# Order of the turns inside a group of weight chunks, and another table of modulation sums, in a two-block transformer kernel

## The chip, the cores and the metric

The kernel runs on one core of one Trainium2 chip. The metric is device time in microseconds (us) of one execution. Five engines work side by side: PE (TensorE, matrix multiplication), DVE (VectorE), ACT (ScalarE), POOL (GpSimd) and SP (SyncE, which here only issues the loads of weights). They share data through on-chip buffers and wait for each other on semaphores. Each engine executes its own instructions strictly in the order in which they are written, so an instruction that waits holds up everything behind it.

## The reference

Two transformer blocks on 256 tokens of width 2048, in float32. The first:

```
mod = silu(c) @ w_ada + b_ada                     # 2048 x 12288: six vectors: shifts, scales, gates
h = modulate(rms_norm(x), sh_a, sc_a)             # the same for the 256 context tokens
qa, kva, kr, cb, cc, ch = split(h @ w_in)
att = attention(8 heads, keys of x and of the context)      # softmax, q and k through low-rank products
conv = cb * dwconv3(cc * ch)                      # depthwise over three neighbouring tokens
x = x + gt_a * (rms_norm(concat(att, conv)) @ w_out)
hf = modulate(rms_norm(x), sh_f, sc_f)
u = dwconv3(hf @ w_up); a, g = split(u)
x = x + gt_f * ((a * silu(g)) @ w_down)
```

The second block has two other attentions of 8 heads each, a gated merge and a squared-ReLU MLP of width 8192. The time is that of streaming some 550 MB of weights through PE.

## The kernel before

**Weights in chunks.** SP loads a weight as chunks of 512 KB (2 tiles of 128 rows, 512 columns each) into the ring `raw` of 8 slots. A matrix product in float32 accuracy is made of three products of reduced precision: ACT rounds a chunk into `whi` (`split`, L613), DVE computes `wlo = raw - whi` (`split`, L1093), and PE multiplies `whi` by the rounded activations, `whi` by their rest, and `wlo` by the rounded ones (`block`, L1869 to L1871). `whi` and `wlo` have rings of 4 slots (`NSPLIT`), so ACT can be at most four chunks ahead of PE. A chunk is 24 matmuls of 256 columns.

**Groups.** A product of 512 output columns is a group of 8 chunks (some have 6 or 4). While PE multiplies group k, ACT and DVE already split group k+1. Both walk it in a function `ahead(group, between, later, sums, side, third)` of their own. Its loop over the chunks n puts other work of these engines ahead of a chunk's split:

- `between`, at n = 4: the output of group k is taken out of PE's accumulator (the line that copies or scales `half`), with what follows directly.
- `later`, at n = 6: the rest of its treatment, such as `gated` (SiLU gate and product into `hid`) in the first block's FFN.
- `side[n]`: one step of work that runs in the background. `att1` is a step of the first attention: on DVE the maximum over a head's scores (L1457) and sometimes a `mix` (L1462), on ACT the squares of an older head's output (L828), a copy (L833), the exponential (L837), and the scaled copy of an older head's output (L843).
- `sums`: after the split of chunk n, `sum_chunks` takes so many chunks of `w_ada` and adds them, scaled by silu(c), to `acc` (DVE L1120 or L1122 for one half and L1125 for the other). Eight of them make 512 modulation values. PE then reduces `acc` over the partitions (`mod`, L1840) and DVE's `mod` adds them to `mod_f`.

The attention is a round trip: PE computes a head's scores into one bank (L2122, L2123), DVE takes the maximum (L1457), ACT the exponential into `tmp` (L837), and only then may PE compute the next scores. The root that scales a head (POOL L575 to L583) starts from L828's sum and ends at ACT's L843. PE does these steps between two products' chunks.

**Stages.** To about 140 us `w_ada`'s first third and the norm, from 140 to 555 us the projections, convolution and first attention, to 601 us the rest of `w_out` and the FFN's norm (`ffn_norm` on DVE, in the group that carries UP_SUMS[0]), to 975 us the 16 products with `w_up` that stand in straight code, then loops: the other `w_up` products and `w_down`. The second block starts at about 1380 us. The remaining two thirds of `w_ada`'s chunks are summed in the stages between; 32 of them in the `w_up` stage, by the table `UP_SUMS` (one tuple for each product, one number for each chunk n). `UP_MODS` says after which products' gates DVE adds the four finished sums. The same tables set the order in which SP loads, since `raw` is one ring for all.

Of the kernel before, what the change touches and what calls it, by code (L numbers as in the profile page):

```python
# [16 lines left out]
GC = KT // KC  # L17
# [151 lines left out]
FIRST_TILES = (8, 9, 10, 11, 0, 1, 2, 3, 12, 13, 14, 15)  # L169
LAST_TILES = (4, 5, 6, 7)  # L170
WIDE_SUMS = (2, 1, 1, 2, 1, 1)
LIGHT, HEAVY, NONE = (0, 0, 1, 1, 0, 0, 1, 1), (0, 0, 0, 1, 0, 0, 0, 0), (0,) * GC
UP_SUMS = [NONE] + [LIGHT, HEAVY] * 6 + [(0, 0, 1, 1, 0, 0, 0, 0)] + [NONE] * 2
UP_MODS = (8, 16, 20, 28)
FILLS = [("x", tb, q) for tb in range(2) for q in range(4)] + ["roots"] + \
    [("ctx", tb, q) for tb in range(2) for q in range(4)] + ["vec a", "vec b"]
FILL_AT = list(range(10, 18)) + [33] + list(range(38, 46)) + [46, 47]
# [10 lines left out]
def program(nc, ins, consts, out, known, traced):  # L188
    with ExitStack() as ctx:
# [216 lines left out]
        def _(sp):  # L406
# [71 lines left out]
            def up_group(c0, sums):  # L478

                for c, count in enumerate(sums):  # L480
                    load(W["w_up"], KC * c, KC, c0, GW)
                    load_mod(count)

            for t in range(0, 2 * HT, 4):
                up_group(t * P, UP_SUMS[t // 2])
                up_group(FFN + t * P, UP_SUMS[t // 2 + 1])

# [115 lines left out]
        def _(act):  # L603
# [3 lines left out]
            def split(elems):  # L607

                act.wait_ge(raw_in[L.raw_slot()], L.loads())
                if L.n.get("hi_ready", 0) >= NSPLIT:  # L610
                    act.wait_ge(s_chunk_used, L.at("hi_ready", 1 - NSPLIT))
                s, c = L.split_slot(), L.raw_slot()
                A(whi[:, s, 0:elems], raw[:, c, 0:elems], ACT.Copy).then_inc(s_hi_ready, 1)  # L613
                L.mark("hi_ready")
                L.add("drained")
# [13 lines left out]
            def per(sums, n):  # L629
                return sums if isinstance(sums, int) else sums[n]  # L630

            def ahead(group, between=None, later=None, sums=0, side=None, third=None, split=split):


                L.end = L.n.get("hi_ready", 0)
                chunks = group
                for n, elems in enumerate(chunks):
                    if third and n == third[0]:
                        third[1]()
                    if side and n in side:  # L640
                        next(side[n], None)
                    if n == 4 and between:
                        between()
                    if n == 6 and later:
                        later()
                    split(elems)
                    L.add("drained", per(sums, n))
                if len(chunks) <= 4 and between:
                    between()
                if len(chunks) <= 4 and side and 4 in side:  # L650
                    next(side[4], None)
                if len(chunks) <= 6 and later:
                    later()
# [38 lines left out]
            def norm(name, src, dst, shift=None, known=False, after=None):  # L692
                if not known:
                    squares(flat(src), after=after)
                    root(T, rstd[:, 0:T], D)
                round_tiles(name, KT, lambda k: dst[:, k, 0:T], shift)


            for name in ("c", "c_ctx", "b_ada"):
                g, r, n = VEC_AT[name]  # L700
# [192 lines left out]
            def into_ffn(g):  # L893
                turn()
                act.wait_ge(s_half_read, L.at("half_read"))
                square_x(g)

            def ffn_root():
                root_of(rstd[:, 0:T], sum_bank[:, 0:T], D, ("sq", L.n["squared_x"] - 1), "ffn")

            ahead(LAST, turn)
            for g in range(3):
                ahead(LAST, lambda: into_ffn(g))
            ahead(STD, lambda: (into_ffn(3), ffn_root(), norm("hf", xt, hf, lambda k: mod_f[:, 16 + k:17 + k], True)), None, UP_SUMS[0])

# [6 lines left out]
            def up(side, tile, nb=4):  # L912

                turn()
                act.wait_ge(s_half_read, L.at("half_read"))
                for b in range(nb):
                    taps(("ffn_conv_w1", "ffn_conv_b"), tile + (FT * side + b), b, conv_y[side][:, b, :], side)
# [14 lines left out]
            for t in range(0, 2 * HT, 4):  # L932
                ahead(STD, lambda: up(0, t), None, UP_SUMS[t // 2 + 1])
                ahead(STD, lambda: up(1, t), lambda: gated(t // HT, t % HT), UP_SUMS[t // 2 + 2] if t < 2 * HT - 4 else 0)
            with L.loop(2):
# [67 lines left out]
            for s in range(4):  # L1003
                before = att[s - 1] if s > 0 else None
                side = [{} if before is None else d for d in ({6: before}, {1: before, 4: before, 6: before}, {1: before, 4: before})]
# [78 lines left out]
        def _(dve):  # L1084
# [44 lines left out]
            def per(sums, n):  # L1129
                return sums if isinstance(sums, int) else sums[n]  # L1130

            def ahead(group, between=None, later=None, sums=0, side=None, third=None, split=split):


                L.end = L.n.get("hi_ready", 0)
                chunks = group
                for n, elems in enumerate(chunks):
                    if third and n == third[0]:
                        third[1]()
                    if side and n in side:  # L1140
                        next(side[n], None)
                    if n == 4 and between:
                        between()
                    if n == 6 and later:
                        later()
                    split(elems)
                    sum_chunks(per(sums, n))
                if len(chunks) <= 4 and between:
                    between()
                if len(chunks) <= 4 and side and 4 in side:  # L1150
                    next(side[4], None)
                if len(chunks) <= 6 and later:
                    later()
# [102 lines left out]
            for g in range(8):  # L1256
                ahead(STD, mod_rows if g > 0 else None, (lambda: mod_cols(4 * g - 4)) if g > 0 else None,
                      side={c: replies[GC * g + c] for c in range(GC) if GC * g + c in replies})
# [254 lines left out]
            def both(*parts):  # L1513
                for part in parts:
# [8 lines left out]
                  side={1: att1, 3: rotate(3), 4: conv_normed(1, 0), 5: both(conv_normed(1, 1))}, third=(1, lambda: keys(3)))  # L1523
# [8 lines left out]
            def into_ffn(g):  # L1532
                onto_x(4 * g, mix_gate)
                L.add("squared_x")
# [13 lines left out]
            for g in range(1, 3):  # L1548
                ahead(LAST, lambda: into_ffn(g))
            ahead(STD, ffn_norm, None, UP_SUMS[0])  # L1550

# [23 lines left out]
            for t in range(0, 2 * HT, 4):  # L1575
# [3 lines left out]
                ahead(STD, lambda: up(1, t),  # L1579
                      lambda: (gated(t // HT, t % HT, 4, key), mod() if t + 4 in UP_MODS else None), 0 if last else UP_SUMS[t // 2 + 2])  # L1580
            with L.loop(2) as i:
# [123 lines left out]
            for s in range(4):  # L1705
# [3 lines left out]
                      side={2: roots()} if s == 0 else {1: before, 4: before, 6: before})  # L1709
                ahead(STD, lambda: (times(k2[:, s % 2, :, :], rr, ("k", s)), token_roots() if s == 0 else None),  # L1710
                      (lambda: norm_x(0 if s == 0 else 3)) if s < 2 else None,
                      side={} if s == 0 else {1: before, 4: before})
# [103 lines left out]
        def _(pe):  # L1816
# [399 lines left out]
            for t in range(0, 2 * HT, 4):  # L2216
                product(of(hf), ready=(lambda n: ("hf", n)) if t == 0 else None, with_mod=t in UP_MODS, sums=UP_SUMS[t // 2])
                product(of(hf), sums=UP_SUMS[t // 2 + 1])
# [167 lines left out]
```

## Time and profile before

| | before |
|---|---|
| runs | 2724.72, 2726.81 and 2737.24 us, median 2726.81 |
| execution that was profiled | 2737.24 us, its span 2735.5 us |
| PE busy | 2643.3 us, 97% of the span |
| DVE busy | 1737.7 us, 64% |
| ACT busy | 1224.1 us, 45% |
| POOL busy | 110.0 us, 4% |
| chain that ended last | PE 87%, DVE 7%, ACT 2%, POOL 1% |

The profiled execution is the slowest of the three, 10.4 us above the median. Busy time is a sum over stages with different limits, and PE counts as busy at half clock as well. The chain that ended last is followed back from the last instruction: at each step to what released it.

### The profile page before, as it was taken

How to read it: one execution, taken by the hardware profiler on the slowest of the kernel's cores; microseconds unless marked ns; L12 is line 12 of the kernel's file. 1: busy time of each engine (PE TensorE's matmuls, PEld its weight loads, DVE VectorE, ACT ScalarE, POOL GpSimd, SP SyncE). 2: the span in 40 equal slices, each digit the busy share in tenths (PEclk: the TensorE clock that was granted, in tenths of full speed). 3: DMA queues.
4: the chain of work that ended last, by engine and by line, in shares of the span. 5: the costliest groups of instructions: out<-in, count | busy, mean ns of one | idle time of the engine just before them, and what ended most of it. 6: DMA issues, size and time to landing. Idle time of an engine off the chain costs nothing.

```text
span 2735.5 us, 51222 instructions
## 1 busy us (share of the span) xinstructions
PE 2643.3 (97%) x21440; PEld 2560.4 (94%) x21440; DVE 1737.7 (64%) x2020; ACT 1224.1 (45%) x1487; POOL 110.0 (4%) x196
## 2 busy tenths in 40 slices
PE   6899988989999999999999999999999999999998
PEld 4699877889999999999999999999999999999997
DVE  5988676777888755665564555555555555555554
ACT  6743333345454544444543444444444444434433
POOL 0000323300000000000000010000000000000000
PEclk9999999999999999999998999999999999999999
DMA  9877766747777655465564555666556656666662
GB/s 355 276 233 263 244 207 206 244 165 239 250 237 251 212 190 185 155 222 180 172 193 132 163 161 162 193 188 198 184 178 194 194 193 195 194 193 190 196 208 100
DMA packets 289064, 553.56 MB, mean 202 GB/s; under 512 B 19386, under 2 KB 28712, under 8 KB 288232
## 3 DMA queue, kind: packets, MB, share of 16 engines
q1 hardware_dynamic: 288328, 548.53, 61.9%
q8 instruction: 142, 2.33, 0.3%
q10 hardware_dynamic: 544, 2.29, 0.2%
q14 instruction: 50, 0.41, 0.0%
HBM read 548.53 MB, written 2.10 MB: 201 GB/s over the span
## 4 chain that ended last, share of the span: by engine, by line
PE 87%; DVE 7%; ACT 2%; issue 2%; POOL 1%; DMA 1%; SPq 0%; ACTq 0%; DVEq 0%; POOLq 0%
PE half L1869 26%; PE half L1870 26%; PE half L1871 26%; DVE wlo L1093 3%; PE half L1903 1%; PE half L1905 1%; PE half L1904 1%; PE half L2162 1%; ACT whi L613 1%; DVE acc L1122 1%; DMA raw<-in_w_ada 1%; DVE acc L1125 1%; PE half L2123 0%; PE half L2150 0%; PE half L2122 0%
## 5 line engine op out<-in xcount | busy, mean ns | idle before, releaser
L1093 DVE TENSOR_TENSOR wlo<-raw,whi 128x1024 fp32r<-128x1024 f32 (+1 forms) x909 | 1090.9, 1211 | 829.8 <-ACT whi L613 827.3
L613 ACT ACTIVATE whi<-raw 128x1024 fp32r<-128x1024 f32 (+1 forms) x909 | 942.2, 1049 | 1077.6 <-PE half L1871 946.7
L1869 PE MATMUL half<-hf,whi 128*128 128x256 f32 x2400 | 670.3, 279 | 6.2 <-DVE hf L1185 5.1
L1870 PE MATMUL half<-hf,whi 128*128 128x256 f32 x2400 | 668.8, 279 | 0.0
L1871 PE MATMUL half<-hf,wlo 128*128 128x256 f32 x2400 | 668.8, 279 | 0.0
L1869 PE MATMUL half<-hid,whi 128*128 128x256 f32 x1712 | 475.6, 278 | 0.0
L1871 PE MATMUL half<-hid,wlo 128*128 128x256 f32 x1712 | 475.0, 277 | 0.0
L1870 PE MATMUL half<-hid,whi 128*128 128x256 f32 x1712 | 474.9, 277 | 0.0
L1869 PEld LDWEIGHTS half<-hf,whi 128*128 128x128 f32 x2400 | 452.5, 189 | 7.7 <-issue 5.8
L1870 PEld LDWEIGHTS half<-hf,whi 128*128 128x128 f32 x2400 | 453.2, 189 | 0.0
L1871 PEld LDWEIGHTS half<-hf,wlo 128*128 128x128 f32 x2400 | 453.1, 189 | 0.0
L1869 PE MATMUL half<-h,whi 128*128 128x256 f32 x1520 | 431.7, 284 | 5.1 <-issue 3.8
L1870 PE MATMUL half<-h,whi 128*128 128x256 f32 x1520 | 425.8, 280 | 0.0
L1871 PE MATMUL half<-h,wlo 128*128 128x256 f32 x1520 | 425.4, 280 | 0.0
L1871 PEld LDWEIGHTS half<-hid,wlo 128*128 128x128 f32 x1712 | 322.8, 189 | 0.0
L1869 PEld LDWEIGHTS half<-hid,whi 128*128 128x128 f32 x1712 | 321.7, 188 | 0.1
L1870 PEld LDWEIGHTS half<-hid,whi 128*128 128x128 f32 x1712 | 321.6, 188 | 0.1
L1869 PEld LDWEIGHTS half<-h,whi 128*128 128x128 f32 x1520 | 289.5, 190 | 7.1 <-issue 4.6
L1870 PEld LDWEIGHTS half<-h,whi 128*128 128x128 f32 x1520 | 290.0, 191 | 0.6 <-issue 0.2
L1871 PEld LDWEIGHTS half<-h,wlo 128*128 128x128 f32 x1520 | 289.6, 190 | 0.0
L1125 DVE SCALAR_TENSOR_TENSOR acc<-raw,silu_sb,acc 128x512 f32<-128x512 f32 x128 | 96.2, 752 | 4.5
L1122 DVE SCALAR_TENSOR_TENSOR acc<-raw,silu_sb,acc 128x512 f32<-128x512 f32 x112 | 84.3, 753 | 12.0 <-DVE wlo L1093 0.5
(284 smaller groups left out, 3064.7 us busy)
## 6 DMA issues: line engine op xcount, KB each, us to landing
raw<-in_w_up SPq DMA_DIRECT2D x288, 512.0 KB, 4.4
raw<-in_w_in SPq DMA_DIRECT2D x216, 512.0 KB, 4.0
raw<-in_w_down SPq DMA_DIRECT2D x212, 512.0 KB, 4.7
raw<-in_w_ada SPq DMA_DIRECT2D x192, 512.0 KB, 5.3
raw<-in_w_out SPq DMA_DIRECT2D x64, 512.0 KB, 5.0
raw<-in_w_proj_a SPq DMA_DIRECT2D x16, 512.0 KB, 4.3
raw<-in_w_proj_b SPq DMA_DIRECT2D x16, 512.0 KB, 4.1
raw<-in_w_up SPq DMA_DIRECT2D x16, 384.0 KB, 3.4
```

The costliest lines, as they stand in the source:

```text
L613: A(whi[:, s, 0:elems], raw[:, c, 0:elems], ACT.Copy).then_inc(s_hi_ready, 1)
L1093: V.tensor_tensor(wlo[:, s, 0:elems], raw[:, c, 0:elems], whi[:, s, 0:elems].bitcast(F32), ALU.subtract).then_inc(s_drained, 1)
L1122: V.scalar_tensor_tensor(a, w[:, 0, :], s[:, 0:1], a, ALU.mult, ALU.add).then_inc(s_dve_step, 1)
L1125: V.scalar_tensor_tensor(a, w[:, 1, :], s[:, 1:2], a, ALU.mult, ALU.add).then_inc(s_drained, 1)
L1869: mm(o, hi, x[:, 0:T], start=(k == 0 and b % 2 == 0), stop=False, skip_group_check=True)
L1870: mm(o, hi, x[:, T:2 * T], start=False, stop=False, skip_group_check=True)
L1871: return mm(o, lo, x[:, 0:T], start=False, stop=(k == nk - 1), skip_group_check=True)
L1903: mm(o, xh, hi, start=(k == 0), stop=False)
L1904: mm(o, xh, lo, start=False, stop=False)
L1905: ins_ = mm(o, xl, hi, start=False, stop=(k == nk - 1))
L2162: ins_ = mm(sum_bank[:, i * T:(i + 1) * T], ones[:], sq[:, n % 2, b * T:(b + 1) * T], start=(first and i + b == 0), stop=(last and b == 3) ...
```

## The change

Three edits. In the tables, the 32 `w_ada` chunks of the `w_up` stage are spread otherwise: before, products in pairs had four chunks (at n = 2, 3, 6, 7) and one (at n = 3), from the second group on; after, each of the first ten groups has three (at n = 1, 3, 5), the eleventh two, and the last five none. The group of `ffn_norm` is the first of them and had none before. `UP_MODS` follows. In ACT's `ahead`, the background step `side[n]` stands behind `between` and `later` where it stood ahead of both. In DVE's, it stands behind `between`, still ahead of `later`. PE's and POOL's functions are as they were.

```diff
-LIGHT, HEAVY, NONE = (0, 0, 1, 1, 0, 0, 1, 1), (0, 0, 0, 1, 0, 0, 0, 0), (0,) * GC
-UP_SUMS = [NONE] + [LIGHT, HEAVY] * 6 + [(0, 0, 1, 1, 0, 0, 0, 0)] + [NONE] * 2
-UP_MODS = (8, 16, 20, 28)
+UP_SUMS = [(0, 1, 0, 1, 0, 1, 0, 0)] * 10 + [(0, 1, 0, 0, 0, 1, 0, 0)] + [(0,) * GC] * 5
+UP_MODS = (8, 12, 16, 24)
 # ACT, ahead():
                     if third and n == third[0]:
                         third[1]()
-                    if side and n in side:
-                        next(side[n], None)
                     if n == 4 and between:
                         between()
                     if n == 6 and later:
                         later()
+                    if side and n in side:
+                        next(side[n], None)
                     split(elems)
 # DVE, ahead():
                     if third and n == third[0]:
                         third[1]()
+                    if n == 4 and between:
+                        between()
                     if side and n in side:
                         next(side[n], None)
-                    if n == 4 and between:
-                        between()
                     if n == 6 and later:
                         later()
```

The changed file is one line shorter above all functions, so its line numbers are those of before less one. The edits to `ahead` take effect where a group has both a turn at n = 4 and `side[4]`.

DVE, in the group whose turn is `conv_in(4)` (about 397 us; `convt` and `zpad` are the convolution's buffers), before:

```order
L1125 SCALAR_TENSOR_TENSOR acc<-raw,silu_sb,acc 128x512
L1457 TENSOR_REDUCE stat<-half 128x1
L1462 SCALAR_TENSOR_TENSOR mix<-half,vec,mix 128x256
L1159 TENSOR_TENSOR zpad<-half,sq 128x4x256
L1380 MEMSET stat 128x1
L1385 SCALAR_TENSOR_TENSOR convt<-zpad,vec,convt 128x256 x4
L1390 SCALAR_TENSOR_TENSOR convt<-zpad,vec,convt 128x256 x4
L1093 TENSOR_TENSOR wlo<-raw,whi 128x1024
```

The same place after:

```order
L1124 SCALAR_TENSOR_TENSOR acc<-raw,silu_sb,acc 128x512
L1158 TENSOR_TENSOR zpad<-half,sq 128x4x256
L1379 MEMSET stat 128x1
L1384 SCALAR_TENSOR_TENSOR convt<-zpad,vec,convt 128x256 x4
L1389 SCALAR_TENSOR_TENSOR convt<-zpad,vec,convt 128x256 x4
L1456 TENSOR_REDUCE stat<-half 128x1
L1461 SCALAR_TENSOR_TENSOR mix<-half,vec,mix 128x256
L1092 TENSOR_TENSOR wlo<-raw,whi 128x1024
```

The maximum over the scores, and with it the round trip to PE, moved behind ten convolution instructions. On ACT the four taps of the convolution moved ahead of the attention's step in the same place. In the group that starts at about 300 us (turn `conv_in(2)`), ACT has before:

```order
L828 ACTIVATE r,stat<-half 128x128
L833 ACTIVATE sq<-half 128x512
L837 ACTIVATE tmp,stat<-half,stat 128x512
L843 ACTIVATE r<-half,stat 128x128
L794 ACTIVATE zpad<-convt 128x4x256
```

and after:

```order
L793 ACTIVATE zpad<-convt 128x4x256
L827 ACTIVATE r,stat<-half 128x128
L832 ACTIVATE sq<-half 128x512
L836 ACTIVATE tmp,stat<-half,stat 128x512
L842 ACTIVATE r<-half,stat 128x128
```

The copy into `zpad` moved ahead of the whole attention step; on DVE the `convt` product moved ahead of the maximum there. In three other places such turns change places: one copy of a `row` at about 87 us, the values `vt` at about 456 us, and in the second block q, k, v and the gate's sigmoid against steps of its attentions.

DVE at the end of `ffn_norm`'s group and in the first group with a gate (`hid`), in the `w_up` stage, has after the change:

```order
L1092 TENSOR_TENSOR wlo<-raw,whi 128x1024 x2
L1121 SCALAR_TENSOR_TENSOR acc<-raw,silu_sb,acc 128x512
L1124 SCALAR_TENSOR_TENSOR acc<-raw,silu_sb,acc 128x512
L1553 COPY zpad<-half 128x4x256
L1357 SCALAR_TENSOR_TENSOR sq<-zpad,vec,sq 128x256 x4
L1362 SCALAR_TENSOR_TENSOR sq<-zpad,vec,sq 128x256 x4
L1092 TENSOR_TENSOR wlo<-raw,whi 128x1024 x2
L1119 TENSOR_SCALAR acc<-raw,silu_sb 128x512
L1124 SCALAR_TENSOR_TENSOR acc<-raw,silu_sb,acc 128x512
L1158 TENSOR_TENSOR sq<-sq 128x1024
L1158 TENSOR_TENSOR hid<-sq,hid 128x4x256
```

where before the two `wlo` were followed directly by the gate:

```order
L1554 COPY zpad<-half 128x4x256
L1358 SCALAR_TENSOR_TENSOR sq<-zpad,vec,sq 128x256 x4
L1363 SCALAR_TENSOR_TENSOR sq<-zpad,vec,sq 128x256 x4
L1093 TENSOR_TENSOR wlo<-raw,whi 128x1024 x2
L1159 TENSOR_TENSOR sq<-sq 128x1024
L1159 TENSOR_TENSOR hid<-sq,hid 128x4x256
```

A summed chunk (n = 5) now stands between the turn and the gate, in five of the eight groups that have a gate.

## Rows read from the trace of the kernel before

**Rows 1.** The page: busy time of PE, and the chain by engine.

```profile
PE 2643.3 (97%) x21440; PEld 2560.4 (94%) x21440; DVE 1737.7 (64%) x2020; ACT 1224.1 (45%) x1487; POOL 110.0 (4%) x196
PE 87%; DVE 7%; ACT 2%; issue 2%; POOL 1%; DMA 1%; SPq 0%; ACTq 0%; DVEq 0%; POOLq 0%
```

**Rows 2.** Timeline of DVE from 392 us: start, duration, instruction [idle before].

```profile
397.17 0.68 DVE L1457 TENSOR_REDUCE stat<-half 128x1 f32<-128x512 f32 x1
400.66 1.22 DVE L1159 TENSOR_TENSOR zpad<-half,sq 128x1024 f32<-128x1024 f32 x1
...
406.25 1.22 DVE L1093 TENSOR_TENSOR wlo<-raw,whi 128x1024 fp32r<-128x1024 f32 x1
```

**Rows 3.** Timeline of ACT from 392 us.

```profile
394.26 0.25 ACT L828 ACTIVATE r<-half 128x128 f32<-128x128 f32 x1
...
397.89 0.69 ACT L837 ACTIVATE tmp<-half,stat 128x512 f32<-128x512 f32 x1 [2.80 <-DVE stat L1457]
...
399.49 0.37 ACT L843 ACTIVATE r<-half,stat 128x128 f32<-128x128 f32 x1 [0.82 <-POOL stat L583]
...
402.03 2.08 ACT L789 ACTIVATE convt<-zpad,vec 128x256 f32<-128x256 f32 x4 [1.81 <-DVE stat L1380]
```

**Rows 4.** Timeline of PE from 398 us.

```profile
398.73 2.08 PE L2122 MATMUL half<-ktt,qall 128*128 128x512 f32 x2 [4.87 <-ACT tmp L837]
```

**Rows 5.** A window by engine: length, busy (instructions), granted clock, DMA share, GB/s.

```profile
397.00:407.20 10.20, 8.47 (x25) 5.47 (x26) 7.00 (x14) 6.21 (x13) 2.99 (x8) 0.50 0.32 99
```

**Rows 6.** Timeline of DVE from 300 us.

```profile
303.67 0.68 DVE L1457 TENSOR_REDUCE stat<-half 128x1 f32<-128x512 f32 x1
304.27 1.21 DVE L1159 TENSOR_TENSOR convt<-half,convt 128x1024 f32<-128x1024 f32 x1
```

**Rows 7.** Timeline of ACT from 300 us.

```profile
301.11 0.28 ACT L828 ACTIVATE r<-half 128x128 f32<-128x128 f32 x1 [3.92 <-PE half L2150]
...
304.39 0.69 ACT L837 ACTIVATE tmp<-half,stat 128x512 f32<-128x512 f32 x1 [2.42 <-DVE stat L1457]
...
305.99 0.37 ACT L843 ACTIVATE r<-half,stat 128x128 f32<-128x128 f32 x1 [0.82 <-POOL stat L583]
306.25 1.05 ACT L794 ACTIVATE zpad<-convt 128x1024 f32<-128x1024 f32 x1
```

**Rows 8.** Timeline of PE from 306 us.

```profile
306.79 1.02 PE L2122 MATMUL half<-ktt,qall 128*128 128x512 f32 x2
```

**Rows 9.** Timeline of DVE from 585 us, in the norm's group.

```profile
588.35 1.22 DVE L1093 TENSOR_TENSOR wlo<-raw,whi 128x1024 fp32r<-128x1024 f32 x1 [2.03 <-ACT whi L613]
589.50 0.15 DVE L1159 TENSOR_TENSOR mod_f<-half,vec 128x4 f32<-128x4 f32 x1
...
596.90 1.75 DVE L1543 RECIPROCAL rstd<-rstd 128x256 f32<-128x256 f32 x1 [5.47 <-ACT rstd L799]
```

**Rows 10.** Timeline of DVE from 646 us, in the first group with a gate.

```profile
649.78 1.23 DVE L1093 TENSOR_TENSOR wlo<-raw,whi 128x1024 fp32r<-128x1024 f32 x1 [1.60 <-ACT whi L613]
651.11 0.75 DVE L1122 SCALAR_TENSOR_TENSOR acc<-raw,silu_sb,acc 128x512 f32<-128x512 f32 x1
...
652.57 1.22 DVE L1554 COPY zpad<-half 128x1024 f32<-128x1024 f32 x1
...
663.88 4.63 DVE L1093 TENSOR_TENSOR wlo<-raw,whi 128x1024 fp32r<-128x1024 f32 x4
```

**Rows 11.** Timeline of ACT from 646 us.

```profile
648.69 1.06 ACT L613 ACTIVATE whi<-raw 128x1024 fp32r<-128x1024 f32 x1 [1.77 <-PE half L1871]
```

**Rows 12.** Windows, L1869 alone: length, PE busy (matmuls), PEld busy, clock, DMA.

```profile
844.00:891.00 47.00, 38.12 (x138) 25.82 (x138) 1.00 0.73 244
931.00:1154.00 223.00, 177.20 (x630) 118.29 (x630) 1.00 0.56 181
1160.00:1297.00 137.00, 111.20 (x403) 75.62 (x403) 1.00 0.58 197
```

**Rows 13.** The window at half clock, columns as in rows 5.

```profile
1485.90:1503.00 17.10, 17.10 (x81) 17.10 (x82) 2.94 (x6) 2.05 (x4) 0.00 (x0) 0.50 0.30 95
```

## The prediction

> **What bounds the kernel now.** I read the page first. PE is busy for 2643.3 us, 97% of the span, and the chain that ended last lies on PE for 87%, on DVE for 7% [rows 1]. So DVE's and ACT's orders cost nothing as long as PE finds its next chunk ready, and the change can act in three ways only: where PE runs dry while it waits for DVE or ACT, where the rounds of the attention make it wait, and by the pace of its own matmuls. I then went to each place where the order of the two engines differs, and read DVE, ACT and PE there side by side.
>
> The worst is at 397 us. The chain there is DVE's maximum at 397.17, ACT's exponential at 397.89, PE's scores at 398.73, and PE had idled 4.87 us for it [rows 2 to 4]. The reader is to see that a single short instruction, well placed, ends a stall of PE, and that `conv_in(4)` stood behind it, from 400.66 on, where nobody waited for it.
>
> **The place at 397 us.** `conv_in(4)` now goes first. On DVE it takes from 400.66 to 406.25, 5.6 us, taps of ACT included [rows 2]; its input is there, since PE had ended the product before it turned idle (398.73 - 4.87 = 393.9) [rows 4]. The maximum moves from 397.17 to about 402.8, the exponential to 403.5, the scores to 404.3: PE's stall grows from 4.9 to 10.5 us. On ACT the taps come before the attention's step, and the square sum L828 can't start before they end: 397.17 + (402.03 - 400.66) + 2.08 = 400.6 instead of 394.26. From L828 to the scaled copy L843 it was 5.2 us [rows 3], so L843 comes at 405.8, 1.5 us behind the scores where before it was 0.8 behind: some 0.5 us more may show. I take **+5.6**. Bounds: 0 if the product in front were later than I think and PE had no turn there, 7 if L843 is late as well. The split behind it comes at 407 instead of 406.3, and it is for a chunk that PE reaches some chunks later. The half clock after the stall was 10.2 us [rows 5]: granted 0.50, that is 1.2 GHz, behind an idle stretch of 4.9 us. A longer idle stretch before it need not lengthen what follows the restart; I add **0.5**, between 0 and 4.
>
> **The place at 304 us.** PE took up the scores at 306.79 without a wait [rows 8]. DVE's `convt` (1.21 us) now precedes the maximum, 303.67 becomes 304.9, and ACT's `zpad` copy, which needs `convt`, holds L828 to L843 back until 305.9 [rows 6, 7]. The exponential starts at about 306.85 and lasts 0.69, scores at 307.7: +0.9. Worse, L828 moves from 301.11 to 305.9, L843 was 4.9 behind it, so it comes at 310.8 where it was 305.99, and PE's turn for that head follows the scores by 3 us. PE waits there 1.4 us more. **+2.3**, bounds 0 and 5.
>
> **Other exchanges.** At 456 us `vt` (1.2 us) goes ahead of work behind which DVE idled long for PE; at 87 us a row copy exchanges with a product of equal rank; in the second block the steps of the attention are turned against 1.2 us copies where I found no wait of PE at all. **0** for all, bounds -1 and +2; the cover is the four split chunks that PE has in hand.
>
> **The norm's group.** The group of `ffn_norm` had no sums, and has two before the turn. DVE idled 2.03 us before the split at 588.35, which hides the first. The second falls between that split and `mod_f` at 589.50, and from there everything is serial: squares, root on ACT, reciprocal at 596.90, `hf`, PE [rows 9]. A summed chunk costs DVE 652.57 - 651.0 = 1.6 us with its issue [rows 10]. **+1.6**, bounds 0 (if the sum fell into the wait as the first does) and 3.
>
> **The gated groups.** In the first group with a gate, ACT's split of chunk 3 starts at 648.69, released by PE's end of the group before [rows 11]. So PE needs chunk 6 six chunks later. A chunk is 24 matmuls of 223 / 1890 = 0.118 us, 2.83 us [rows 12], which gives 665.7. DVE starts that split (the first of the four at 663.88) and ends it at 665.1 [rows 10]: between them stand the turn, two splits, the gate. With the semaphores the margin is some 0.3 us. The change puts one more sum between, 1.6 (1.4 where it is the first of eight). Followed in the same way, the five gated groups that get it have margins of 0.3, 0.9, 0.3, 1.1 and 1.4. Stalls: 1.1 + 0.7 + 1.3 + 0.5 + 0.2 = 3.8, and what the pairs before had too much in the ungated groups gives 0.3 back, while a stall in one group moves the ring for the next; I take **+4**, bounds 0 and 8. It is no matter of loads: eleven chunks of 0.52 MB in 22.6 us are 255 GB/s, and where 244 GB/s were moved the share of the DMA engines was 0.73 [rows 12], so it becomes 0.76.
>
> **PE's pace.** At full clock PE has two paces. From 931 to 1154 us there are 630 matmuls of one line out of three in 223 us, 0.1180 us each; from 844 to 891 us 138 in 47 us, 0.1135; and from 1160 to 1297 us 403 in 137 us, 0.1133 [rows 12]. The granted clock is 1.00 in all three. The pace changes only where the stream is interrupted: by the sums' matmuls (L1840) at four places in the `w_up` stage, or by a stall. Four such places gave fast, slow, fast, slow, and the last one holds for 223 us. Of the 553 us from 601 to 1154, 111 were fast (89 about the stretch of the row, and 22 from 705 on, found in the same way). The change moves these places to products 4, 6, 8 and 12 and adds stalls, so the draw is made anew. All slow costs 111 x (0.118 / 0.1133 - 1) = +4.6; all fast gains 442 x 0.04 = -17. The largest stake is the stretch behind the last place, some 260 us or 10 us. I take half of it: **-5**.
>
> By the Trainium skill (TensorE: Matmul & The Clock Gate, Back-to-back issue gap) isolated back-to-back matmuls are N / 2.4 + 2.5 ns apart at the full clock, one value for 256 columns, 109 ns. The rows have 113 and 118 at the same granted clock, so the page doesn't give the second pace; were one rate all there is, this term would be 0 and the time 2741.
>
> **Sum.** 5.6 + 0.5 + 2.3 + 0 + 1.6 + 4 - 5 = +9.0. The profiled execution took 2737.24 us, but 17.1 us of it ran at half clock with PE busy all through and no stall before [rows 13], 8.5 us lost. Without it: 2728.7, 1.9 above the median of 2726.8; I set the sum against the median: **2736 us**.
>
> **Rivals.** (a) *The pace falls to slow and stays.* Place: behind the last sums, product 12, at about 895 us. If the stream restarts slow there and in the earlier pieces, the term is +4.6 instead of -5 and the time 2726.8 + 14.0 + 4.6 = 2745, slower. It decides as soon as less than about 130 us of the 553 run fast. For it: 442 of 553 us were slow. Against: 630 us further on are fast for long after interruptions of the same kind.
> (b) *The round trips are absorbed.* PE has work between its attention steps, and a stall of one round shortens the next: L843 or the next wait comes with its own slack. Then 304 and 397 us cost 2 together, the gates 1, the norm 0: 2726.8 + 3 - 3 = 2727. For it: after the place at 397 there are further waits that another engine sets. Against: those are set by PE's own progress and move along.
> (c) *The pace is fast from the norm on.* -17 instead of -5, 2724; with (b) besides, 2712.
> (d) *The stalls cost more than their length.* Each of the gated stalls resets the pace or takes the clock to 0.50 for as long as at 397 us, 4 us a time at one or two places, and L843's lateness is carried: 2750.
>
> **How the numbers follow.** Forecast 0.43; (a) 0.24; (b) 0.14; (c) 0.11, a third of it below 2713; (d) 0.08. About 0.5%, 13.6 us, is what a measurement of this kernel can tell from no change: faster means under 2713.2, slower over 2740.4. Slower: (a) and (d) wholly or nearly, 0.30. Faster: the third of (c) and a little of (b), 0.06. The rest, 0.64, is the same. Range: 2721 to 2749, which leaves about 0.08 on each side; the forecast's own is 2730 to 2741.
>
> **What would show it.** PE's wait for the exponential at about 404 us should be 10 to 11 us, DVE's maximum there behind the convolution. At about 311 us PE should wait for L842. DVE's `mod_f` in the norm should stand 1.6 us later after the split than now. The gated groups should show gaps of 0.2 to 1.3 us before PE's chunk 6. The interval of PE's matmuls behind 895 us tells the pace. I am wrong if the wait at 404 us is still 5 us, if the time until 601 us is not 9 to 10 us longer, or if between 601 and 1160 us the difference is outside -13 to +9.

## The result, and the profile after

| | before | after |
|---|---|---|
| median | 2729.4 us (4 runs, 2724.7 to 2737.2) | 2751.2 us (4 runs, 2749.6 to 2753.3) |
| profiled execution, span | 2737.2, 2735.5 us | 2751.8, 2749.9 us |

The fourth run of before, 2732.0 us, was not known when the forecast was made. The ratio is 1.0078, with a 95% interval of 1.0051 to 1.0104. The forecast was 2736 us in a range of 2721 to 2749: the time lies 2 us above the range. The page of the changed kernel has PE at nearly the busy time of before and a larger part of the chain on DVE, 9% against 7 [rows 1]:

```profile
PE 2646.2 (96%) x21440; PEld 2561.8 (93%) x21440; DVE 1738.6 (63%) x2020; ACT 1224.0 (45%) x1487; POOL 102.9 (4%) x196
PE 84%; DVE 9%; ACT 2%; issue 2%; DMA 1%; POOL 1%; SPq 0%; ACTq 0%; DVEq 0%; POOLq 0%
```

**At 397 us** DVE's timeline shows the convolution ahead of the maximum, which answers to [rows 2]:

```profile
398.34 1.22 DVE L1158 TENSOR_TENSOR zpad<-half,sq 128x1024 f32<-128x1024 f32 x1
...
403.93 0.68 DVE L1456 TENSOR_REDUCE stat<-half 128x1 f32<-128x512 f32 x1
```

ACT's timeline has the exponential right behind it, and the scaled copy L842 1.4 us behind the exponential [rows 3]; PE's timeline has the wait, 8.7 us where it was 4.9 [rows 4]:

```profile
404.65 0.69 ACT L836 ACTIVATE tmp<-half,stat 128x512 f32<-128x512 f32 x1 [2.13 <-DVE stat L1456]
...
406.10 0.37 ACT L842 ACTIVATE r<-half,stat 128x128 f32<-128x128 f32 x1 [0.67 <-POOL stat L582]
```

```profile
405.48 1.22 PE L2121 MATMUL half<-ktt,qall 128*128 128x512 f32 x1 [8.68 <-ACT tmp L836]
```

From the start of `zpad` to that of the maximum it is 5.6 us, the term of the sum to the tenth.

**At 304 us** PE waits for the scores, which it did not before [rows 8]:

```profile
304.48 0.70 PE L2121 MATMUL half<-ktt,qall 128*128 128x512 f32 x1 [3.73 <-ACT tmp L836]
```

For the scaled copy L842, for which the forecast had a second wait there, PE did not wait: ACT's row is the first of these, PE's the second.

```profile
306.50 0.37 ACT L842 ACTIVATE r<-half,stat 128x128 f32<-128x128 f32 x1 [2.07 <-POOL stat L582]
308.45 0.42 PE L2139 MATMUL half<-ident_sb,r 128*128 128x128 f32 x1
```

**In the norm's group** a summed chunk stands between the split and `mod_f`, and DVE's idle time before the split went from 2.03 to 0.94 us [rows 9]:

```profile
596.06 1.23 DVE L1092 TENSOR_TENSOR wlo<-raw,whi 128x1024 fp32r<-128x1024 f32 x1 [0.94 <-ACT whi L612]
597.39 0.75 DVE L1121 SCALAR_TENSOR_TENSOR acc<-raw,silu_sb,acc 128x512 f32<-128x512 f32 x1
...
598.85 0.15 DVE L1158 TENSOR_TENSOR mod_f<-half,vec 128x4 f32<-128x4 f32 x1
```

From the split to `mod_f` it is 2.8 us, where it was 1.15. PE's wait for ACT's squares in the norm grew by the same 1.6 us, here before and then after:

```profile
PE half L2162 <- ACT sq L885: 3.6, 1, 3.6
PE half L2161 <- ACT sq L884: 5.2, 1, 5.2
```

**In the gated groups** PE waits for `wlo` five times from 603 to 900 us, where before had no such wait at all. PE's waits there:

```profile
PE half L1868 <- DVE wlo L1092: 3.1, 5, 0.9
```

So a stall of PE stands at each of the four places that the prediction named. At 304 us the second wait that it had there is missing. To see what the places cost in all I cut both traces at the same matmul of PE; each trace has 21,440 of them, in the same order but for those of L1840. Since PE has two paces, I also price every fast matmul as a slow one: I add 0.0045 us for each that runs at 0.1133 us. I call this the priced time. Two priced times of the same stretch differ by waits and half clock only. Later executions of the same two kernels are in the table as well (labels are those of the experiments below); the columns are the stretches by before's clock.

```
               127-   284-   388-   456-   584-   602-    fast matmuls  profiled
               284    388    456    584    602    1160    in all        execution, us
before         159.0  105.6   68.3  129.9   17.7  562.7   12368         2737.2
e1, same       157.4  105.5   68.3  129.5   17.7  563.0   11864         2737.0
e16, same      159.0  105.8   64.5  129.5   17.1  562.7   11704         2735.4
after          157.8  111.0   72.4  130.0   19.3  567.5   12094         2751.8
e5, same       157.4  107.7   71.5  127.9   19.3  565.9   11873         2746.8
e13, same      157.1  107.9   72.8  130.0   19.3  568.0   13481         2743.5
e14, same      156.8  107.9   71.5  128.9   19.2  567.3   12998         2744.6
e15, same      157.1  104.7   73.1  129.5   19.3  567.7   11842         2746.9
mean after
- mean before   -1.3   +2.2   +5.3   -0.3   +1.8   +4.5
```

Behind 1160 us the priced times are 255.5 and 1053.6 us in all eight for two stretches, and 298.9 to 302.2 for the one between.

### The profile page after: what moved, and what is told of

Its sections match the earlier page's. It is cut to its first block, busy times and chain, and to the rows that moved or that the text cites. A ratio compares the mean times of both kernels' runs of the same rounds, so it can differ in the third digit from the quotient of the medians.

```text
span 2749.9 us, 51222 instructions
## 1 busy us (share of the span) xinstructions
PE 2646.2 (96%) x21440; PEld 2561.8 (93%) x21440; DVE 1738.6 (63%) x2020; ACT 1224.0 (45%) x1487; POOL 102.9 (4%) x196
## 4 chain that ended last, share of the span: by engine, by line
PE 84%; DVE 9%; ACT 2%; issue 2%; DMA 1%; POOL 1%; SPq 0%; ACTq 0%; DVEq 0%; POOLq 0%
PE half L1868 25%; PE half L1869 25%; PE half L1870 25%; DVE wlo L1092 3%; DVE acc L1121 1%; DMA raw<-in_w_ada 1%; ACT whi L612 1%; PE half L1902 1%; PE half L1904 1%; PE half L1903 1%; DVE acc L1124 1%; PE half L2161 1%; PE half L1991 0%; PE half L2122 0%; PE half L2149 0%
## 5 line engine op out<-in xcount | busy, mean ns | idle before, releaser
L1869 PE MATMUL half<-hf,whi 128*128 128x256 f32 x2400 | 667.5, 278 | 0.0
L1869 PE MATMUL half<-hid,whi 128*128 128x256 f32 x1712 | 476.1, 278 | 0.0
L1868 PEld LDWEIGHTS half<-hf,whi 128*128 128x128 f32 x2400 | 452.3, 188 | 11.3 <-issue 5.8
L1869 PEld LDWEIGHTS half<-hf,whi 128*128 128x128 f32 x2400 | 451.8, 188 | 0.0
L1869 PE MATMUL half<-h,whi 128*128 128x256 f32 x1520 | 425.4, 280 | 0.0
L1869 PEld LDWEIGHTS half<-hid,whi 128*128 128x128 f32 x1712 | 321.4, 188 | 0.1
L1869 PEld LDWEIGHTS half<-h,whi 128*128 128x128 f32 x1520 | 289.7, 191 | 0.6 <-issue 0.2
L1121 DVE SCALAR_TENSOR_TENSOR acc<-raw,silu_sb,acc 128x512 f32<-128x512 f32 x112 | 84.3, 753 | 11.7
```

The costliest lines, as they stand in the source:

```text
L1121: V.scalar_tensor_tensor(a, w[:, 0, :], s[:, 0:1], a, ALU.mult, ALU.add).then_inc(s_dve_step, 1)
L1868: mm(o, hi, x[:, 0:T], start=(k == 0 and b % 2 == 0), stop=False, skip_group_check=True)
L1869: mm(o, hi, x[:, T:2 * T], start=False, stop=False, skip_group_check=True)
```

## The experiments

For each, the ratio is to runs of before made in the same session, with its 95% interval. "Priced" stands for the priced time of a stretch of the table. S and P are the two theories of the expectations: the time was lost in stalls (S), or in the pace of PE's matmuls (P).

**e1 and e16: before again.**

> The kernel before once more, for a second profile of it. Theory S (stalls): the change lost about 14 us in stalls of PE, and the two profiles of before and after (2737.2 and 2751.8) differ by just these 14.5 us; a second profile of before then has the same paces of PE in the same stretches (slow from 931 to 1154 us, 0.118 us a matmul, fast from 1160 to 1297, 0.113). Theory P (pace): the paces are drawn anew in each execution, which is why before spans 2724.7 to 2737.2 us; then the second profile has other stretches fast, and its time differs from 2737.2 by 0.0045 us for every matmul of another pace. The half clock of 17 us at about 1486 us, which I took for an accident: S and P alike, it is there again if it belongs to the program (the changed kernel shows 13.7 us of it in the same place), and gone if my prediction was right.

> The kernel before, a third profile: by P1 and P2 alike fast behind the last sum with a chance of 3 in 8.

Medians 2732.6 (12 runs, 2721.7 to 2737.0; ratio 1.0006, 0.9992 to 1.0020) and 2732.1 us (8 runs). The windows of e1 behind the last sum and in the loop after it, L1869 alone:

```profile
926.00:1152.00 226.00, 179.74 (x641) 120.10 (x640) 1.00 0.58 179
1154.00:1296.00 142.00, 113.00 (x402) 75.46 (x402) 1.00 0.59 191
```

The second is 142 / (3 x 402) = 0.1177 us for a matmul, and the same instructions of the same kernel ran at 0.1133 in the first profile [rows 12]. So the pace is drawn anew in each execution; up to 1409 us this one draw makes 5.8 us. Theory P is right in this. And the half clock at 1486 us is there again, PE busy all through it:

```profile
1486.00:1503.00 17.00, 17.00 (x81) 17.00 (x82) 2.52 (x5) 2.61 (x4) 0.00 (x0) 0.50 0.30 97
```

All 18 profiles have it there or a few us beside, 13.7 to 20.5 us long. It is no accident of the one execution [rows 13], and the 8.5 us that the prediction took off for it were wrong.

**e2: the tables alone.**

```diff
-UP_SUMS = [NONE] + [LIGHT, HEAVY] * 6 + [(0, 0, 1, 1, 0, 0, 0, 0)] + [NONE] * 2
-UP_MODS = (8, 16, 20, 28)
+UP_SUMS = [(0, 1, 0, 1, 0, 1, 0, 0)] * 10 + [(0, 1, 0, 0, 0, 1, 0, 0)] + [(0,) * GC] * 5
+UP_MODS = (8, 12, 16, 24)
```

> Only the tables UP_SUMS and UP_MODS are changed, the order inside the groups is that of before. Theory S: the time to the norm is that of before, the norm's group costs 1.7 us (in the two profiles the step from the product before the norm to the one after it grew by that), the gated groups' stalls some 4 us: +6, ratio 1.002. Theory P: in the changed kernel's profile PE ran at the slow pace from the last sum on to 1425 us, and in that of before it was fast from 1160 to 1297 and in one piece behind it; if the place of the last sum does that, this kernel has it too and costs 6 us more, +12, ratio 1.0045.

Ratio 1.0038 (1.0024 to 1.0051), +10.4 us. Priced: 19.3 in the norm's stretch and 567.7 in the next, 1.8 and 4.9 more than before, and 105.6 and 68.3 ahead of them, as before. So the tables own these two terms, and neither of the other two. The loop from 1160 was fast, against P. The time lies 4 us above S's 6, just outside the interval's half width of 3.6, and 1.6 below P's 12; the priced stretches leave no room for more stalls. What is left is the pace of the runs without a profile, which no trace shows; the profiled run itself had more fast matmuls than before's first.

**e3: the order alone, on both engines.**

> Only the order inside the groups is changed (both engines), the tables are those of before. Theory S: all of the 9 us that are lost before 601 us, of which about 4 at the place at 304 us and 4 at the place at 397 us, and nothing behind: +8 to +9, ratio 1.003. Theory P: the same stalls, and on top of them other paces behind; the time is then anywhere from -8 to +5 beside it.

Ratio 1.0043 (1.0028 to 1.0058), +11.7 us. Its edit is the diff of the two `ahead` functions. Priced: 108.0 and 70.1, then 17.7 and 562.5: the loss is ahead of 601 us and nothing behind. PE's wait for the scores at 304 us is 0.7 us here, by its timeline:

```profile
305.17 1.13 PE L2122 MATMUL half<-ktt,qall 128*128 128x512 f32 x2 [0.69 <-ACT tmp L837]
```

That is the 0.9 of the prediction; in the changed kernel's first profile it was 3.7. The windows tell why: here PE was granted 0.53 of its clock ahead of the place,

```profile
292.00:299.00 7.00, 6.87 (x19) 3.89 (x20) 5.67 (x7) 2.91 (x4) 0.00 (x0) 0.53 0.88 293
```

so it reached the scores later and waited less. In the changed kernel's first profile the clock fell behind the longer wait instead:

```profile
305.00:312.00 7.00, 7.00 (x25) 4.96 (x24) 3.91 (x5) 3.12 (x6) 2.28 (x6) 0.54 0.24 73
```

Of the other profiles with the new order there, e6, e8, e11 and e12 also have 111 us for this stretch, e5, e7, e13 and e14 have 107.7 to 107.9 like e3, and e15 has 104.7. The old order has such draws too. In e4 and e9, where no half clock came ahead of the place, PE waited 1.5 us at these scores, and the stretch took about 107 us in e4, 104 in e9 and 108 in e10. So the two ranges overlap, and only their means, some 3 us apart over seven and eleven profiles, tell the order's part. By the wait alone it is 2.2 us without half clock ahead (3.7 against 1.5), and 0.5 to 0.7 with it. The order on one engine alone was not tried: as the program is written, the two would wait for each other for ever. With DVE alone in the new order its maximum stands behind work that needs taps which ACT has behind this maximum's exponential; with ACT alone in it DVE's L1462, ahead of `zpad`, waits for ACT's L848, which stands behind the taps of that `zpad`.

**e4: the place at 397 us alone.** In before, a parameter makes both engines take the new order in the group of `conv_in(4)`.

```diff
-    ahead(STD, lambda: conv_in(4), ..., side={..., 4: att1, 6: att1})
+    ahead(STD, lambda: conv_in(4), ..., side={..., 4: att1, 6: att1}, new=True)
```

> Only the group whose turn is conv_in(4), at 397 us, has the new order on both engines; everything else is before. Theory S, by the prediction: PE's wait for the exponential grows from 4.9 us to 10.5, +5.6. By the changed kernel's profile, where the step over this place grew by 4.0 us: +4. A rival: the time that PE loses here is given back at the next wait, which another engine's chain sets: 0.

Ratio 1.0020 (1.0009 to 1.0031), +5.5 us. Priced, 388 to 456 us took 70.2, against 68.3, 68.3 and 64.5 in before. It costs, so the rival falls; whether 4 or 5.6 the interval can't tell. PE waited 7.4 us at the scores there, 3 less than forecast. Half clock explains the gap: it came at 377.8 us for 6.8 us, so PE reached the scores some 3.4 us later than at full clock (an estimate from these 6.8 us), while the wait ended when DVE's maximum and the exponential were done. Sorted by how long PE was at half clock just ahead of the place (between 377 and 391 us), the waits of all profiles with these two orders are, in us:

| half clock just ahead | old order at 397 us | new order |
|---|---|---|
| none | 4.7 to 4.9 (before, e1, e2) | 10.3 (e15) |
| 3.4 us | 3.1 (e11) | 8.7 to 8.9 (after, e5 to e8, e13, e14) |
| 6.8 us | 1.6, 1.8 (e16, e12) | 7.2, 7.4 (e3, e4) |

In each row the new order has 5.4 to 5.8 us more. PE's line in e15:

```profile
399.39 2.08 PE L2121 MATMUL half<-ktt,qall 128*128 128x512 f32 x2 [10.27 <-ACT tmp L836]
```

**e11 and e12: the place at 304 us alone, and the changed kernel without the one at 397.** The same parameter, in e11 at `conv_in(2)` of before; e12 is the changed kernel with the old order at `conv_in(4)`.

> Only the group whose turn is conv_in(2), at 304 us, has the new order on both engines. Theory S: the stretch 284 to 388 us, 105.6 us at the slow pace in before, becomes 107.9 where PE was at half clock just ahead of the place (as in e3_order and e7_norm_free), and 111 where it was not (as in the changed kernel's profile); at 601 us less of it is left, since DVE, which sets the time of the scores at 397 us, was late by only 1.2: +1 to +3. Rival: it adds fully: +2.3 to +5.4.

> The changed kernel with only the group at 397 us in the order of before. Theory S: the step from 388 to 405 us is 17.7 us again instead of 21.7, and 601 us is reached 4 to 5.6 us earlier; the stretches behind are those of the changed kernel (567.5 us from the norm to the loops, at the slow pace). Rival (the wait is given back later): no difference at 601 us.

e11: ratio 1.0015 (1.0003 to 1.0028), +4.1 us. Priced 111.0 and 65.7: 5.4 more than before in the stretch of the change and less in the next. e12: ratio 1.0050 (1.0037 to 1.0063), 5 runs; 111.0 and 64.9, against 111.0 and 72.4 in the changed kernel. The step from 388 to 405 us is 11.2 us here, as in e16 (11.3), where the two other profiles of before have 17.6. The reader is to see two things. Of the 7 us between e12 and the changed kernel the order at 397 us makes some 5.6, by the table of waits, for e12 had 6.8 us of half clock ahead of the place and the changed kernel's first profile 3.4. And what PE loses ahead of 397 us is in part taken back there, because PE waits for DVE anyway. But e12's median is not below the changed kernel's (ratio 1.0042 in e5): on the whole time this undoing can't be seen.

**e5, e13, e14, e15: the changed kernel again.**

> The changed kernel once more, for a second profile and the spread of its times. Counted by the number of the matmul, and with every fast matmul (0.1133 us) priced as a slow one (0.1178), the changed kernel's profile is 13 to 15 us longer than the two of before: this part I call the stalls. The medians differ by 21.8. Theory P1: the rest of some 7 us is the pace, drawn from the same distribution as before; five runs in 3.7 us were chance, and more runs of the same kernel scatter over some 15 us as those of before do, with a median of about 2745. Theory P2: in the changed kernel the long stretch behind the last sum's matmuls (896 to 1169 us, 2316 matmuls, 10 us between the paces) is slow in all or nearly all executions; then the runs stay between 2746 and 2755 and the second profile is slow there too.

> The changed kernel, a third profile. P2: slow (0.118 us a matmul) all through the stretch behind the last sum. P1: fast with a chance of 3 in 8.

> The changed kernel, a fourth profile: slow behind the last sum by P2, fast with a chance of 3 in 8 by P1.

> The changed kernel, a fifth profile: slow behind the last sum by P2, fast with a chance of 3 in 8 by P1.

Medians 2744.7 (11 runs, 2737.9 to 2748.9), 2746.3 (8), 2744.8 (7) and 2747.2 us (4); ratios 1.0042 (1.0026 to 1.0059), 1.0045 (1.0032 to 1.0058), 1.0037 (1.0018 to 1.0055) and 1.0039 (0.9995 to 1.0083). So over 30 more runs the change costs 10 to 12 us, not 21.8. The first four after lie 4 to 6.5 us above these medians; those of before, 2729.4, are among the medians of their later sessions, 2728.4 to 2734.8. The 11 runs of e5 scatter over 11 us, as P1 has it. The stretch behind the last sum was slow in all five profiles of the changed kernel. Its windows in the first one:

```profile
897.00:1168.00 271.00, 215.56 (x768) 143.94 (x767) 1.00 0.58 181
```

0.1176 us for a matmul. Over all kernels: with the last sum in product 12, slow in 9 of 9 profiles; with it in product 14 fast in 3 of 9 (e3, e4, e10). In e10:

```profile
932.00:1146.00 214.00, 173.68 (x631) 118.19 (x630) 1.00 0.61 187
```

0.1130 us. None of nine would come in 3 cases of 100 if the chance were one in three; but were the chance the same for both kinds, all three fast ones would still fall among the same nine in 10 cases of 100, so P2 may hold and is not shown.

**e6: the third sum behind the gate.**

```diff
-UP_SUMS = [(0, 1, 0, 1, 0, 1, 0, 0)] * 10 + [(0, 1, 0, 0, 0, 1, 0, 0)] + ...
+UP_SUMS = [(0, 1, 0, 1, 0, 0, 0, 1)] * 10 + [(0, 1, 0, 0, 0, 0, 0, 1)] + ...
```

> The changed kernel with each product's third sum moved from n = 5 to n = 7, behind the gate. Theory S: the gated groups' stalls go (the stretch from the norm to the loops, priced at the slow pace, is 567.6 us in both kernels with the new tables and 562.5 to 563.1 in the four of before's tables): 563 here, time 4 to 5 us less than that of the changed kernel. Rival: the stalls come from having three sums in every gated group, not from where they stand: 567.

Priced, 602 to 1160 us took 562.9 instead of 567.5, and PE's waits there shrank from five and 3.1 us to

```profile
PE half L1868 <- DVE wlo L1092: 0.2, 1, 0.2
```

with the same three sums in the same groups. It is the place of the sum between turn and gate, as the prediction had it. In the whole time (ratio 1.0040, 1.0024 to 1.0057) the 4.6 us don't show: the profile had 11296 fast matmuls, 800 fewer than the changed kernel's first, which is 3.6 us.

**e7: no sums in the norm's group.**

```diff
-UP_SUMS = [(0, 1, 0, 1, 0, 1, 0, 0)] * 10 + [...] + [(0,) * GC] * 5
-UP_MODS = (8, 12, 16, 24)
+UP_SUMS = [(0,) * GC] + [(0, 1, 0, 1, 0, 1, 0, 0)] * 10 + [...] + [(0,) * GC] * 4
+UP_MODS = (8, 16, 20, 24)
```

> The changed kernel with the tables one group later, so that the group of the FFN's norm has no sums. Theory S: the step over the norm (584 to 601 us in before) is 17.7 us again instead of 19.3, and the rest as in the changed kernel. Rival: the 1.6 us came from the half clock, which is split in two pieces there in both kernels with the new tables (592 and 602 us): then the half clock is still in two pieces and the step 19.3.

The stretch fell from 19.3 to 16.6 us, and DVE's timeline has `mod_f` directly behind the split again, at 588.91 and 590.05. The half clock there is in one piece in this profile, so a part of the 2.7 us may be the clock's, and this single run doesn't exclude the rival. e12 does: it has the sum there, and its half clock is in one piece, 17.1 us from 590.2; it still took 19.3 us, and PE's wait for ACT's squares was 5.2 us as in the changed kernel. All profiles with the sum have 19.2 to 19.3, those without it at most 17.7.

**e8: PE's last sum in product 14.** `UP_MODS = (8, 12, 16, 28)` in the changed kernel.

> The changed kernel with PE's reduction of the last 512 sums in product 14 instead of 12, as before has it, and nothing else. In stalls it changes nothing. Theory P2: the pace behind the last sum is decided at that interruption and what precedes it; at product 12 it came out slow, at 14 it is fast in about half of the executions, as in before's family (slow in two profiles, fast in two): the runs scatter over 10 us or more and the median falls by 3 to 7 us. Theory P1: same distribution as the changed kernel, median within 2 us of it.

Ratio 1.0049 (1.0033 to 1.0065), median 2745.8, the stretch slow in its profile: as P1 has it, and no gain.

**e9 and e10: the opposite order.** In before, both engines take the attention's step ahead of the convolution's at n = 3; e10 also takes DVE's step in the group of `onto_x(0)` at n = 0.

```diff
-    side={0: conv_normed(0, 0), 1: att1, 3: conv_normed(0, 1), 4: att1, 6: att1}
+    side={0: conv_normed(0, 0), 1: att1, 3: first_then(att1, conv_normed(0, 1)), 6: att1}
 # e10, DVE, onto_x(0):
-    side={1: att1, 3: att1, 5: both(att1)}
+    side={0: att1, 3: att1, 5: both(att1)}
```

> The kernel before, with the opposite of what the change does at 397 us: on both engines the attention's step of n = 4 is put ahead of conv_normed(0, 1) at n = 3. Theory S: DVE's maximum, at 397.17 us in before, comes at about 392, the exponential before PE ends the product at 393.6, so PE's wait of 4.9 us there goes, and with it part of the 10.2 us at half clock behind it (up to 4 us): stretch 388 to 456 us, 68.3 us at the slow pace in before, becomes 60 to 64; -4 to -8 in all. Rival: the wait only moves to the next head or to the convolution's roots: 0.

> As e9_att_first, and in the group whose turn is onto_x(0) DVE's attention step stands at n = 0 instead of n = 1 (ACT's stays). Theory S: PE's longest wait for the exponential, 7.4 us at 470 us in before, is for a maximum at 476.5 that stands behind a split and two summed chunks; it comes 4 us earlier, the wait falls to about 3.6 us: another -4. Rival: ACT's L843, whose root starts at 470.5 and takes 5 us, sets the end: -2.

e9: ratio 0.9991 (0.9980 to 1.0003); e10: 1.0002 (0.9990 to 1.0014). The wait at 397 us is gone, 388 to 405 us took 9.4 us instead of 17.6. But the whole stretch to 456 us, 64.5 to 68.3 us in before, took 67.0 (64.9 in e10), for the wait moved. PE's waits of e9 from 385 to 480 us:

```profile
PE half L2132 <- ACT tmp L837: 7.4, 1, 7.4
PE half L2116 <- POOL conv_root L563: 5.1, 1, 5.1
PE half L1850 <- DVE wlo L1098: 4.5, 1, 4.5
```

The third line is new: PE comes to its sum early and waits for a split that DVE makes behind the convolution. In e10 the wait at 470 us fell from 7.4 to 3.4 us, and the total did not. So there the rivals were right: from 380 to 456 us DVE's own work is the bound, and the order decides only at which wait PE pays. Neither beats before by more than its measurement can tell.

## Why the prediction was right and wrong

**What bounds, and the four stalls: right in the sum.** The sum of the stalls was 5.6 + 0.5 + 2.3 + 1.6 + 4 = 14.0 us. The mean over five profiles after and three before, all priced, is 2.2 + 5.3 + 1.8 + 4.5 - 1.3 - 0.3 = +12.2. Place by place: 304 us 2.3 and measured 2.2; 397 us 6.1 and 5.3; the norm 1.6 and 1.8; the gated groups 4 and 4.5. e2, e3, e4, e6 and e12 put each with its edit. None of the three signs of being wrong came: the wait at 404 us was 8.7 us, the first profile reached 601 us 9.3 us later, and from there to 1160 us it took 1 us more.

**At 304 us the number is right by luck.** The term was 0.9 for the exponential and 1.4 for L843. PE never waited for L843 (L842) there, and by the prediction's own times (310.8, against 307.7 + 3) there was hardly anything to wait for. The exponential came later by the product and the copy ahead of it, 2.3 us in all. Where half clock had held PE up ahead of the place, 0.5 to 0.7 of that showed, the 0.9 of the forecast; where it hadn't, PE waited 3.7 us, 2.2 more than the old order's 1.5 in the same state. The prediction knew only the first case. Over the profiles the stretch changed by anything between -0.9 and +5.4.

**At 397 us the mechanism was right.** The maximum came 5.6 us later behind DVE's own work, and the wait was to be 10.5 us. It was 10.3 in the one profile without half clock just ahead (e15). In the others PE came to the scores late by the half clock and waited as much less, 8.7 to 8.9 us in most. The time of the scores is DVE's, so this shortens the wait and not the stretch: the stretch grew by 5.3, and its values of the two orders don't overlap (64.5 to 68.3 us in six profiles, 70.1 to 73.1 in ten).

**Other exchanges: 0, right.** The stretches from 456 to 584 us and from 1409 us on are unchanged.

**The base: this step failed.** "17.1 us of it ran at half clock [...], 8.5 us lost. Without it: 2728.7." This was the ground for setting the sum against the median of three runs, 2726.8. Every profile of every kernel has this half clock at that place, so nothing was to be taken off, and the three runs had come out low. The medians of before in the five sessions are 2728.4 to 2734.8, and the mean of its 127 runs there is 2731.3 (one of 3627 us left out): the base was 2 to 8 us too low, 4.5 by the mean. The profiled execution would have been too high a base: the profiled executions of before (mean 2736.6) were each the slowest of their own set of 4, 12 and 8 runs, which is not explained. Set against it the sum, 2737.2 + 9.0, gives 2746, inside the range but still 5 us short.

**The pace: this term failed too.** I took -5, half of the stake behind the last sum, without a row that said so. In profiles the changed kernel has 12458 fast matmuls in the mean and before 11979, which is -2.2 us; in the first pair of profiles it is +1.2. Rival (a) named the place, the stretch behind the last sum, and it was slow in all five; but it was slow in all three of before too, so it moved nothing between them. What (a) did not name, the loop from 1160 us on, is a second draw of 5.8 us that I had fixed as fast. With 12.2 - 2.2 = +10.0 the profiled executions agree (10.2).

**Why the measured time is still 2751.** With the base at 2731.3, stalls of 12.2 and a pace of -2.2 the sum would have been 2741, and the 30 later runs have a mean of 2745.8, in two sessions that had before at 2733.4 and 2734.8. The first four runs after lie within 3.7 us, 4 to 6.5 us above the medians of these 30, and their profile has the 111 us of e6, e8, e11 and e12 at 304 us, 3.2 us above its mean, and a slow loop from 1170 on, 5.8. Both were draws that came out high in this profile. That all four unprofiled runs were high as well is not explained by it. Of the 21.8 us between the first medians 10 to 12 come again in later runs; the rest stays open.

**Rivals.** (b), that the round trips are absorbed, falls by e3 and e4. (c) falls: in none of the five profiles after was even half of the stretch from 602 to 1160 us fast. Of (d), stalls that cost more by the half clock, the place at 304 us is a case, 3 us in one draw of two, not 8.

## What to carry to other kernels

Before a part of a profiled execution is called an accident and taken off, a second profile of the same kernel has to show that it is gone; here it was there in all 18. Three runs are too few for a base where runs of one kernel span some 17 us. Where an engine's pace differs from execution to execution, as PE's does here, cut both traces at the same instruction and price the paces alike: a stall of 1.6 us then shows, where the ratio of the whole time has an interval of 3 to 5 us either way. And work that is moved ahead of a round trip costs its full length there, but only as far as the engine that is late is the one that everybody waits for: a delay of another engine just ahead of it is swallowed, as PE's half clock was at 397 us. Waits before and after are to be compared at the same clock ahead of them.

## What was not expected of the hardware

At a granted clock of 1.00 PE's matmuls of 256 columns follow each other at 0.1133 or 0.1178 us, and for the same instructions it is the one in one execution and the other in the next (137 and 143 us for the same 1212 matmuls). In the last stretch of the second block, where PE waits only once, 2.6 us near the end, the number of fast matmuls was the same in every profile (8010, within 1); in the first block, where PE waits for other engines, it was not. The Trainium skill (TensorE: Matmul & The Clock Gate, Back-to-back issue gap) gives the distance of isolated matmuls at the full clock, 109 ns by its formula for 256 columns; for streams with weight loads, as here, it has measured values for 128 and 512 columns only, 81 and 131 ns. The rows here have two distances at 256 columns, both between these two and both above the formula's. What sets the pace was not found.
